# The RWKV states' inputs of even and odd chunks: two banks, alternating, no stop between them

## The reference, cut to what matters

```python
def rwkv7_scan(r, w, k, v, a, bvec):
    decay = jnp.exp(-jnp.exp(w))
    def step(state, inp):
        r_t, d_t, k_t, v_t, a_t, b_t = inp
        sa = jnp.einsum('bhvk,bhk->bhv', state, a_t)
        state = (state * d_t[:, :, None, :] + sa[..., None] * b_t[:, :, None, :]
                 + v_t[..., None] * k_t[:, :, None, :])
        return state, jnp.einsum('bhvk,bhk->bhv', state, r_t)
```

## Time and profile before

| | us |
|---|---|
| median of three runs | 3529.41 |
| the runs | 3529.41, 3529.43, 3525.97 |
| the profiled execution | 3524.7 |
| its span | 3522.9 |
| TensorE busy | 3341.1 (95%) |
| VectorE busy | 1490.8 (42%) |
| ScalarE busy | 1082.6 (31%) |
| GpSimd busy | 395.9 (11%) |

### The profile page before, as it was taken

One profiled execution on the slowest core, in us unless ns is written; L12 is line 12 of the kernel. 1 busy time (PEld: TensorE's weight loads), 2 busy tenths in 40 slices (PEclk: granted clock), 3 DMA queues, 4 the chain that ended last, 5 costly groups with the idle time before them and its releaser, 6 DMA issues. The chain is left out here.

```text
span 3522.9 us, 38396 instructions
## 1 busy us (share of the span) xinstructions
PE 3341.1 (95%) x16568; PEld 2582.1 (73%) x16568; DVE 1490.8 (42%) x2056; ACT 1082.6 (31%) x1619; POOL 395.9 (11%) x386
## 2 busy tenths in 40 slices
PE   6999999889899999999999989999998999999999
PEld 2466666666758888888877766788886888888887
DVE  6256624665444111113346442556543433333333
ACT  4243324334233111112135553233323322222211
POOL 1022202343212000000012000111211100000000
PEclk9999999999999999999999999899998999999999
DMA  5111110000042111112122010000003111110211
GB/s 234 41 60 61 72 39 24 13 13 24 1 153 75 48 48 48 48 36 91 46 72 83 36 37 18 8 1 1 1 1 150 54 48 48 48 48 30 96 44 71
DMA packets 35257, 182.33 MB, mean 52 GB/s; under 512 B 4261, under 2 KB 4261, under 8 KB 21648
## 3 DMA queue, kind: packets, MB, share of 16 engines
q1 hardware_dynamic: 22176, 133.18, 10.6%
q0 software_dynamic: 12912, 46.69, 3.4%
HBM read 161.89 MB, written 17.96 MB: 51 GB/s over the span
## 5 line engine op out<-in xcount | busy, mean ns | idle before, releaser
L537 PE MATMUL ps<-r,r 128*128 128x512 f32 x2656 | 1056.7, 398 | 14.4 <-DVE r L2022 13.2
L538 PE MATMUL ps<-r,r 128*128 128x512 f32 x2656 | 1048.0, 395 | 0.0
L539 PE MATMUL ps<-r,r 128*128 128x512 f32 x2656 | 1047.9, 395 | 0.0
L537 PEld LDWEIGHTS ps<-r,r 128*128 128x128 f32 x2656 | 501.4, 189 | 142.1 <-issue 20.7
L538 PEld LDWEIGHTS ps<-r,r 128*128 128x128 f32 x2656 | 501.7, 189 | 117.2 <-issue 3.0
L539 PEld LDWEIGHTS ps<-r,r 128*128 128x128 f32 x2656 | 501.4, 189 | 115.7
L1407 ACT ACTIVATE ar<-ps 128x512 f32<-128x512 f32 (+3 forms) x330 | 170.1, 541 | 628.1 <-PE ps L1214 119.5
L1369 ACT ACTIVATE r<-ar 128x1024 fp32r<-128x1024 f32 (+1 forms) x170 | 174.4, 1032 | 550.6 <-PE ps L539 510.6
L2015 DVE TENSOR_TENSOR r<-ar,r 128x1024 fp32r<-128x1024 f32 (+1 forms) x170 | 203.8, 1199 | 324.1 <-ACT r L1369 324.0
L527 PE MATMUL ps<-ar 128*128 128x128 f32 (+5 forms) x1844 | 278.0, 314 | 6.4 <-ACT ar L1407 3.3
L527 PEld LDWEIGHTS ps<-ar 128*128 128x128 f32 (+2 forms) x1844 | 218.9, 174 | 57.1 <-issue 31.8
(11 more groups left out here) (286 smaller groups left out, 3561.4 us busy)
## 6 DMA issues: line engine op xcount, KB each, us to landing
ar<-in_w_mod SPq DMA_DIRECT2D x24, 1024.0 KB, 4.8
ar<-in_w_gu SPq DMA_DIRECT2D x22, 1024.0 KB, 4.8
ar<-in_w_up SPq DMA_DIRECT2D x22, 1024.0 KB, 4.8
ar<-in_w_in SPq DMA_DIRECT2D x19, 1024.0 KB, 4.8
ar<-in_w_dn SPq DMA_DIRECT2D x32, 512.0 KB, 3.4
x<-ar POOLq DMA_DIRECT2D x48, 256.0 KB, 2.3
ar<-x POOLq DMA_DIRECT2D x24, 512.0 KB, 7.0
ar<-in_xT POOLq DMA_DIRECT2D x16, 512.0 KB, 13.7
```

Of the source, the lines that this page charges most:

```text
L537: M.matmul(o, whk, hi[k][:, a:a + n], start=k == 0, stop=False)
L538: M.matmul(o, whk, lo_[k][:, a:a + n], start=False, stop=False)
L539: ins = M.matmul(o, wlk, hi[k][:, a:a + n], start=False, stop=k == nk - 1)
```

## The change

On TensorE, the states' inputs of a group are made chunk pair by chunk pair. The even chunk writes one of the group's banks and the odd chunk the other; `mt` of four chunks takes columns 0 to 255 of a bank and `nn` columns 256 to 511. The three matmuls of the two chunks alternate: even, odd, even, odd, even, odd. The stop between the two kinds is gone. Both banks are noted as freed by VectorE's `nn` signal. The count of matmuls stays.

On VectorE, the sum and the product are made once for each bank, with 256 columns (192 for the odd chunks' product), and the results go to every second block of 64 columns in `MT` and `NN`. The signals for `MT` and `NN` come with the second instruction of each.

```diff
-                om = claim(("mt", g_), next_of(BG), (v_state, ("mt", g_)))
-                on = claim(("nn", g_), next_of(BG), (v_state, ("nn", g_)))
-                for n_ in (0, 2, 4, 6, 1, 3, 5, 7):
-                    if n_ == 1:
-                        ins.then_inc(*product(("half", g_)))
-                        pe.wait_ge(*product.last())
-                    Rc = slice(64 * (n_ % 2), 64 * (n_ % 2) + 64)
-                    x0 = (n_ // 2) * 128 + 64 * j
-                    u0 = a0 + (n_ // 2) * 128
-                    M.matmul(om[R, n_ * 64:n_ * 64 + 64], UW[Rc, u0:u0 + 64], Bt[Rc, x0:x0 + 64], start=True, stop=True)
-                    ins = dot(on[R, n_ * 64:n_ * 64 + 64], [(Bt[Rc, x0:x0 + 64], UW[Rc, u0 + 64:u0 + 128]),
-                                                           (Kt[Rc, x0:x0 + 64], Vt[Rc, x0:x0 + 64])])
+                two = [claim(("mn", g_, i), next_of(BG), (v_state, ("nn", g_))) for i in range(2)]
+                for c in range(0, 256, 64):
+                    x0 = 2 * c + 64 * j
+                    u0 = a0 + 2 * c
+                    for what in range(3):
+                        for i, o in enumerate(two):
+                            Rc = slice(64 * i, 64 * i + 64)
+                            if what == 0:
+                                M.matmul(o[R, c:c + 64], UW[Rc, u0:u0 + 64], Bt[Rc, x0:x0 + 64], start=True, stop=True)
+                            elif what == 1:
+                                M.matmul(o[R, 256 + c:320 + c], Bt[Rc, x0:x0 + 64], UW[Rc, u0 + 64:u0 + 128],
+                                         start=True, stop=False)
+                            else:
+                                ins = M.matmul(o[R, 256 + c:320 + c], Kt[Rc, x0:x0 + 64], Vt[Rc, x0:x0 + 64],
+                                               start=False, stop=True)
                 ins.then_inc(*product(("mn", g_)))
...
-                V.tensor_tensor(th(MT[R, :], 64), th(bank(("mt", g_))[R, :], 64),
-                                bc4(IDN[:, 64 * j:64 * j + 64], R, 8, 64), ALU.add).then_inc(*v_state(("mt", g_)))
-                on = bank(("nn", g_))
+                two = [bank(("mn", g_, i))[R, :] for i in range(2)]
+                for i, o in enumerate(two):
+                    ins = V.tensor_tensor(th(MT[R, :])[:, :, 64 * i:64 * i + 64], th(o[:, 0:256], 64),
+                                          bc4(IDN[:, 64 * j:64 * j + 64], R, 4, 64), ALU.add)
+                ins.then_inc(*v_state(("mt", g_)))
                 if hf == 0:
-                    V.tensor_copy(NN[R, 448:512], on[R, 448:512])
-                V.tensor_tensor(
-                    th(NN[R, 0:448], 64), th(on[R, 0:448], 64),
-                    fac[R, hf * 8:hf * 8 + 7].rearrange("p (c t) -> p c t", t=1).to_broadcast([64, 7, 64]),
-                    ALU.mult).then_inc(*v_state(("nn", g_)))
+                    V.tensor_copy(NN[R, 448:512], two[1][:, 448:512])
+                f = fac[R, hf * 8:hf * 8 + 8].rearrange("p (c two) -> p c two", two=2)
+                for i, o in enumerate(two):
+                    ins = V.tensor_tensor(
+                        th(NN[R, :])[:, 0:4 - i, 64 * i:64 * i + 64], th(o[:, 256:512 - 64 * i], 64),
+                        f[:, 0:4 - i, i:i + 1].to_broadcast([64, 4 - i, 64]), ALU.mult)
+                ins.then_inc(*v_state(("nn", g_)))
```

## The result

The changed kernel takes 3511.54 us (median of six runs, 3509.08 to 3516.86) against 3527.69 us for the one before (six runs, 3523.86 to 3529.73), 16 us less. The ratio is 0.9957, with a 95% interval of 0.9944 to 0.9969, which is 11 to 20 us. The forecast was 3514, and 14.3 us less. The profiled execution has a span of 3509.8 us, 13.1 under the 3522.9 of the earlier trace rows.

The account below looks back on a forecast made before the run. TensorE was taken as what everybody waits for in the handovers. Savings of 3 x 2.29 + 2 x 2.45 + 2.5 = 14.3 us, subtracted from 3524.7 and 3529.41, gave 3510.4 and 3515.1; it took 3514, range 3507 to 3521.5 (8 in 10).

Parts of the forecast that it names:

- part 1: TensorE's stop between even and odd chunks in the states' inputs: 0.22 us lost, 12 times, 2.6 us in all.
- part 2: TensorE's states' inputs: alternating row halves overlap fully, 24 pairs at 58 ns; with TensorE alone, 3.1 us a step.
- part 3: VectorE's evacuation of the states' inputs: two more instructions cost 0.13 us a group, 1.47 against 1.34 us in even halves.
- rival (d): VectorE's gapped writes take 1.1 us per 512 columns, an evacuation 2.5 us; 1.4 us saved in all, 3528; chance 0.03.
- part 4: Both PSUM banks freed by VectorE's last instruction, so each group's reading product (L1282) waits; group 1's some 0.6 us late.
- The 0.86: Handover: time in us taken by group 0's share of the sixteen reading-product passes (L1282), of 1.87 for both groups.
- the 18.6 of TensorE alone: Gain in us over the handovers if TensorE alone counted: six times 3.1.
- The sum of 14.3 us: Handovers' total saving: 3 x 2.29 us in even-half steps, 2 x 2.45 in odd ones, 2.5 in the last step.
- Case (e): TensorE's granted clock falls at other places as gaps shift: 4 us either way on any case; no chance of its own.
- (a): States' inputs: row halves do not overlap, only the stop goes; some 2 us slower in all, 3531; chance 0.05.
- (b): States' inputs: each change of row half costs a 0.05 us start-up; 29 us slower in all, 3559; chance 0.03.
- Rival (c): States' inputs overlap, but TensorE can't be fed a pass each 29 ns; at 40 ns 8 us saved, 3521; chance 0.10.

Follow-up runs that it names:

- the run of 24: Changed kernel's banks and VectorE part, no stop, but all 24 even-chunk passes before the 24 odd ones; 3526.87 us against 3527.24 for the kernel before, ratio 1.000.
- The experiment with the other order: Changed kernel, but VectorE empties the even chunks' bank first and frees it at once; 3505.76 us, ratio 0.9946 to the kernel before.
- the runs of 12 and 24: Changed kernel, but the row half changes only after 12 or 24 passes; 3519.75 us and 3526.87 us, ratios 0.9982 and 1.000 to the kernel before.
- the paired products alone: Changed kernel with both groups' outer products (L1208) of the next step also alternating between row halves; 3506.79 us, ratio 0.9948 to the kernel before.
- both edits: Changed kernel with VectorE emptying and freeing bank by bank, plus alternating outer products (L1208); 3507.21 us, ratio 0.9956 to the kernel before.

## Why the prediction was right, step by step

- The stop (part 1) is gone as forecast. Its own worth can't be read alone: together with the new banks and the longer evacuation it came to nothing measurable in the run of 24.
- The alternation (part 2) was the bigger term, and full overlap at 58 ns for two passes held, now over 24 pairs. The Trainium skill (TensorE: Matmul & The Clock Gate, The mechanism) says that matmuls start in strict program order; the prediction estimated some 125 ns for a pair of matmuls from that. The traces disagree: L1273, L1275 and L1278 start 0.117 us apart, four passes each, and in the run of 24 L1270 starts (2301.97) before L527 passes that stand ahead of it (2302.03).
- One detail of part 2 was wrong: I granted group 1 no overlap with group 0, since they have the same row halves. They have different columns, and three passes of each tile did overlap, so the inputs end at T+2.62 and not T+2.84. In even halves it changed nothing, as VectorE was still at group 0; in odd ones VectorE began group 1 at T+3.04 and not at 3.10.
- VectorE's cost (part 3) was right: 1.47 us, and starts 0.34 apart for 256 columns. The gapped writes cost nothing, so rival (d) is out. Group 1's evacuation, which follows at once, took 1.53 in even halves in place of 1.47 and began at T+3.17 in place of 3.13; together that is the 0.1 by which the even handovers were longer than forecast. In odd halves it took 1.39 in place of 1.34 but began at T+3.04 in place of 3.10, so there the two errors cancelled, and the 5.50 against a forecast of 5.51 is in part luck.
- The banks (part 4): the new wait sits where it was put, before L1286 of group 1, with its start at T+4.75 (4.48 in odd halves), 0.70 (0.56) later than 0.86 after group 0's (forecast 0.6). The 0.86 itself, which the prediction took for TensorE's own pace, was by the times already a wait: before, L1282 of group 1 went to the bank that VectorE's L2734 gives free, and it started at T+6.94 (2304.62), 0.06 after the end of that sum (2303.87 + 0.69, below). The forecast is not touched by that, as the later release comes last in it. The experiment with the other order shows that it is the moment of release that counts. The Trainium skill's warning on copies out of PSUM (TensorEngine Tiling (Array Packing), PSUM Bottleneck) fits: the handovers give 14.1 us, not the 18.6 of TensorE alone.

```profile
2303.87 0.69 DVE L2734 TENSOR_TENSOR ar<-ps,ar 64x512 f32<-64x512 f32 x1 [1.54 <-PE ps L527]
```

- The sum of 14.3 us measured 14.1 in the handovers and the last chain. Case (e), the clock, took 1.5 of it in the profile, and shows in what differs between executions. Two readings behind the sum were wrong without harm. There are five handovers of 7.96 us and not six, as the last step has no next product, which the sum allows for. And the earlier steps do not all keep a clock of 1.0: in the trace of before it is at the lower level for 3.4 us in the second step and in the third (from 2405.8 and 2477.5; granted clock 0.57 and 0.76 in the two rows that stand first below), so (e) should have had these episodes in it. The same kernel's second profile has a span of 3503.5 us in place of 3509.8, with the same handovers. Most of that gap lies before the stage, where one execution had a long stretch at the lower clock and the other did not. 22 us of it, first in the first profile and then in the second, stand below the rows of before:

```profile
2405.50:2409.50 4.00, 4.00 (x24) 4.00 (x23) 1.26 (x3) 1.56 (x4) 0.00 (x0) 0.57 0.00 0
2475.00:2482.00 7.00, 6.14 (x40) 5.88 (x40) 3.13 (x7) 3.16 (x7) 1.48 (x1) 0.76 0.01 2
```

```profile
2240.00:2262.00 22.00, 22.00 (x92) 17.04 (x91) 12.29 (x18) 5.69 (x7) 2.81 (x3) 0.50 0.00 0
```

```profile
2240.00:2262.00 22.00, 21.15 (x165) 18.15 (x166) 19.35 (x28) 10.10 (x14) 7.05 (x6) 1.00 0.05 20
```

At 1.00 TensorE gets 165 matmul records done in these 22 us, at 0.50 only 92. The first T of the two profiles lies 6.0 us apart. A spread of 4 us for case (e) was thus too small by itself: these two executions of one kernel differ by 6.3 us in span. That the median came within 2.5 us of the forecast 3514 is therefore in part luck; the handovers are what bears the mechanism out.
- Rivals (a) and (b) are out; but (b)'s start-up is real where a tile pauses, 0.05 us each, and cost the runs of 12 and 24 their last tenths. Rival (c) is out: a pass each 29 ns was kept up for the 2.6 us of the inputs.

## What to carry to other kernels

Matmuls that use half of the rows can run two at a time, but only if the program brings the halves near to each other: here runs of two and of six passes a half kept both halves busy, runs of 24 hardly overlapped at all. Here the halves also had different banks; whether they must is not shown. When TensorE gets faster in a stretch, look next at what takes the results out of PSUM, and release each bank with the instruction that empties it, not with the last of the group. A saving on an engine that then waits is hardly one. Look at the granted clock too: with the paired products alone TensorE was at the lower level for 27 us of the stage in place of 20.5, but with both edits for 17, so one profile does not make a rule of it.

## What the runs showed of the hardware that I had not expected

- TensorE starts a pass for another tile while exactly three passes of the busy tile, which stand ahead of it in the program, are still to come. This was so where the rows change (T+1.22, at the 21st of 24 passes), where the columns change between groups, and with two tiles busy it was three for each.
- From a 64x64 tile's first pass after a pause to its next one it takes 107 ns, and from then on 58.
- Four tiles of 64x64 overlap too: at the change of groups, two tiles drain (L1275, 2298.89) while two others have begun (L1273, 2298.84).
